# Value products with the values as weights, and group norms by transposes, in the first of two transformer blocks

## The chip, the core and the metric

The kernel runs on one core of a Trainium2 chip. The metric is the device time of one execution in microseconds (us). Engines are named as the profile names them: PE (TensorE, with PEld for its weight loads), DVE (VectorE), ACT (ScalarE), POOL (GpSimd), SP (which issues DMAs). Every engine works through its own list in order and waits at semaphores for the others.

## What is computed

Two transformer blocks over 256 tokens of width 1024, in fp32. The change lies in the first block, between its input projection and its output projection:

```python
y_sb = stick_breaking_attention(q_a, k_a, v_a)            # 4 heads of 64, causal
y_ch = chunked_relpos_attention(rms(q_b), rms(k_b), v_b)  # 8 heads of 64, softmax over earlier chunks
y_cv = short_conv_mixer(g_b, g_c, x_c)                    # 256 channels
y = group_rmsnorm(concat([y_sb, y_ch, y_cv]), w)          # groups of 64 features:
#   y * rsqrt(mean(y * y over the 64) + EPS) * w
x = x + y @ w_out
```

Both attentions end in out = A @ v for each head (A is 256 x 256 and lower triangular by blocks of 128, so the upper right block is left out). Then come a feed-forward layer and the whole second block, which the change does not touch.

## The kernel before

All weights stream from HBM in chunks of 128 x 1024 values ("slots", 8 matrix tiles each). ACT rounds each chunk to a high part (wh), DVE forms the remainder (wl), and PE multiplies three times (high by high, high by low, low by high), 24 matmuls of 256 columns a slot in most stages. A ring of 8 chunks lies between the converters and PE.

The program is written by `when(slot, prio, fn)`: for each slot the pieces of work are recorded by rising prio, and each piece appends instructions to the lists of its engines. The slot's own weight matmuls have prio 50, so what has a smaller prio stands ahead of them and what has a larger one behind. Tokens (tok) carry the semaphore counts that later pieces wait for. PSUM is eight banks of 128 x 512 fp32: M[0..2] (pm), S[0..2] (psc), T (ptr), O (po); `claim` waits for the bank's last reader.

The banded attention does one head a slot (slot SC + h and following, SC = 11): scores, row maxima on DVE, exponentials on ACT, three transposes of the probabilities into T (`ch_turn`), a copy to SBUF (`ch_keep`), and the value product (`ch_values`) into O. In it the transposed probabilities are the weights, three tiles of 128 x 128, and the values are what streams, 64 columns each time, so O holds tokens by features. Four heads fill O. `sb_values` is the same for the four causal heads, whose weights swt come from exponentials of S; before them `sb_after` multiplies softplus sums (sph, spl) with a triangle, and waits for the last of sph and spl.

The group norm of a filled O is `group_norm(part, slot, k0)`, for part 0 (heads 0 to 3), part 1 (heads 4 to 7) and part 2 (the causal heads), at slots 18, 22 and 24. `gn_take` copies O to yraw, squares it into sq, sums groups of 64 on DVE, and raises to the power -1/2 on POOL. `gn_scale` multiplies yraw by the factors on DVE. `gn_turn` transposes yraw into T (four transposes), since the output projection wants features by tokens. `gn_split` writes the high part yh (ACT, from T) and the low part yl (DVE, from T). The output projection runs in slots 24 (W1) to 31 and takes the features 2, 3, 4, 5, 0, 1 in that order, then 6 and 7 of the convolution, whose own norm (`cv_sums`, `cv_widen`, `cv_spread`, `cv_done`) already works with transposes of squares and of widened factors. Its bank S[0] is summed in slot 25, its spread in slot 27.

Of the kernel before, what the change touches and what calls it, by code (L numbers as in the profile page):

```python
# [6 lines left out]
P = 128  # L7
# [6 lines left out]
HEAD = 64  # L14
# [156 lines left out]
def build(nc, w, xt, par, cf, cb, rel, wsp, bsp, pos, fin, out):  # L171
# [3 lines left out]
    ALU = mybir.AluOpType  # L175
    ACT = mybir.ActivationFunctionType
    AX = mybir.AxisListType
# [3 lines left out]
    with ctx:  # L181
# [11 lines left out]
        def keep(name, shape, dt=fp32):  # L193
            t, top[0] = put(top[0], name, shape, dt)
            return t
# [8 lines left out]
        def sem(name):  # L204
            return ctx.enter_context(nc.semaphore(name))
# [14 lines left out]
        mhalf = keep("mhalf", [P, 16])  # L220
# [14 lines left out]
        sq = keep("sq", [P, 2, 512])  # L235
        acc = keep("acc", [P, 512])
# [3 lines left out]
        def tiny(width):  # L240
            small_n[0] += 1
            return keep(f"tiny{small_n[0]}", [P, width])
# [6 lines left out]
        gn_ss, gn_f, gn_t, gn_r = tiny(8), tiny(8), tiny(8), tiny(8)  # L249
# [49 lines left out]
        M = [Bank(pm[:, i, :]) for i in range(3)]  # L299
        S = [Bank(psc[:, i, :]) for i in range(3)]  # L300
        T, O = Bank(ptr[:, :]), Bank(po[:, :])

        pe, act, dve, pool, spq = (Lane(sem(n)) for n in ("pe", "act", "dve", "pool", "spq"))
        tok = {}

        def pairs(ap):
            return ap.rearrange("p (a n) -> p a n", a=2)
# [9 lines left out]
        def pcol(name, j):  # L317
            if name == "anw":
                return xa[:, j:j + 1]
            return parm[:, PAR[name] + j:PAR[name] + j + 1]  # L320

        def mm(dst, lhs, rhs, start, stop):
            return lambda e: e.matmul(dst, lhs, rhs, start=start, stop=stop, skip_group_check=True)  # L323

        def tr(dst, src):
            return lambda e: e.transpose(dst, src, cfs[:, CF_ID:CF_ID + P])  # L326

        def scaled(dst, src, scale):
            return lambda e: e.activation(dst, src, ACT.Copy, scale=scale)  # L329

        def func(dst, src, kind, **kw):
            return lambda e: e.activation(dst, src, kind, **kw)  # L332

        def tt(dst, a, b, op):
            return lambda e: e.tensor_tensor(dst, a, b, op)  # L335

        def stt(dst, a, s, b, op0, op1):
            return lambda e: e.scalar_tensor_tensor(dst, a, s, b, op0, op1)

        def ts(dst, a, s1, s2, op0, op1):  # L340
            return lambda e: e.tensor_scalar(dst, a, s1, s2, op0, op1)
# [4 lines left out]
        def when(slot, prio, fn):  # L346
            plan[slot].append((prio, len(plan[slot]), fn))
# [75 lines left out]
        for c in range(4):  # L423
            a = (c % 2) * 1024
            for i in range(2 if c < 2 else 1):
                b = a + (512 if c < 2 else 1024)
# [191 lines left out]
        sq_readers = {0: [], 1: []}  # L618
# [23 lines left out]
        acc_readers = []  # L642
# [215 lines left out]
        SC = VB + 3  # L858
# [47 lines left out]
        def ch_keep(h):  # L906
# [6 lines left out]
            tok["ck", h] = t  # L913
            T.release(t)

        def ch_values(h):
            after = [tok["ck", h], tok["vb", "s"]] + (O.claim() if h % 4 == 0 else [])
            c = (h % 4) * HEAD
            v = vbs[:, :, h * HEAD:h * HEAD + HEAD]
            pt = ptb[:, h % 3, :]  # L920
            pe.quiet(mm(O.ap[:, c:c + 64], pt[:, 0:P], v[:, 0, :], True, True), *after)
            pe.quiet(mm(O.ap[:, 256 + c:320 + c], pt[:, P:256], v[:, 0, :], True, False))
            tok["cp", h] = tok["pv"] = pe.do(mm(O.ap[:, 256 + c:320 + c], pt[:, 256:384], v[:, 1, :],
                                                False, True))

        for h in range(8):
            if h % 2 == 0:
# [7 lines left out]

        def gn_take(part):
            b = part % 2
            used = [tok["gt", part - 2]] if part > 1 else []
            c = act.do(func(yraw[:, b, :], O.ap, ACT.Copy), tok["pv"], *used)
            q = act.do(func(sq[:, b, :], O.ap, ACT.Square), tok["pv"], *sq_readers[b])  # L940
            O.release(q)
            tok["gy"] = c
            t = dve.do(lambda e: e.tensor_reduce(gn_ss[:, :], sq[:, b, :].rearrange(
                "p (h d) -> p h d", d=HEAD), AX.X, ALU.add), q)
            sq_readers[b] = [t]
            if part < 2:
                r = dve.do(lambda e: e.reciprocal(gn_r[:, :], den[:, 8 * part:8 * part + 8]),
                           tok["ce", 4 * part + 3])
                r2 = dve.do(tt(gn_t[:, :], gn_r[:, :], gn_r[:, :], ALU.mult), r)
                t = dve.do(tt(gn_ss[:, :], gn_ss[:, :], gn_t[:, :], ALU.mult), t, r2)  # L950
            t = dve.do(ts(gn_ss[:, :], gn_ss[:, :], 1.0 / HEAD, EPS, ALU.mult, ALU.add), t)
            tok["gf"] = pool.do(tt(gn_f[:, :], gn_ss[:, :], mhalf[:, 0:8], ALU.pow), t)

        def gn_scale(part):
            t = tok["gf"]
            if part < 2:
                t = dve.do(tt(gn_f[:, :], gn_f[:, :], gn_r[:, :], ALU.mult), t)
            v = yraw[:, part % 2, :].rearrange("p (h d) -> p h d", d=HEAD)
            tok["gn"] = dve.do(tt(v, v, gn_f[:, :].unsqueeze(2).to_broadcast([P, 8, HEAD]), ALU.mult),
                               t, tok["gy"])  # L960

        def gn_turn(part):
            after = T.claim() + [tok["gn"]]
            for pj in range(2):
                for tb in range(2):
                    f = tr(T.ap[:, pj * 256 + tb * P:pj * 256 + tb * P + P],
                           yraw[:, part % 2, tb * 256 + pj * P:tb * 256 + pj * P + P])
                    if pj and tb:
                        tok["gt", part] = pe.do(f)
                    else:  # L970
                        pe.quiet(f, *after)

        def gn_split(k0, src, ready, bank):

            for i in range(2):
                a = act.do(scaled(yh[:, k0 + i, :], src[:, i, :], pcol("onw", k0 + i)), *ready)
            for i in range(2):
                t = tok["y", k0 + i] = dve.do(stt(yl[:, k0 + i, :], src[:, i, :], pcol("onw", k0 + i),
                                                  yh[:, k0 + i, :].bitcast(fp32), ALU.mult,
                                                  ALU.subtract), a, *ready)  # L980
            if bank:
                bank.release(t)

        def group_norm(part, slot, k0, wait=0):
            when(slot, 12, lambda: gn_take(part))
            when(slot + 2, 10, lambda: gn_scale(part))
            when(slot + 2 + wait, 65, lambda: gn_turn(part))
            when(slot + 3 + wait, 11, lambda: gn_split(k0, pairs(T.ap), [tok["gt", part]], T))

        group_norm(0, SC + 7, 2, 1)  # L990
        group_norm(1, SC + 11, 4)


        def fm_out(bank, ready, dst, r, rname):
# [84 lines left out]
        def sb_values():  # L1079
            after = O.claim() + [tok["bw", 1], tok["bw", 2], tok["bw", 0], tok["va", "s"]]  # L1080
            for h in range(4):
                c, b, i = h * HEAD, h % 2, h // 2
                v = vas[:, :, c:c + HEAD]
                pe.quiet(mm(O.ap[:, c:c + 64], swt[:, b, i * 256:i * 256 + P], v[:, 0, :], True, True),
                         *after)
                pe.quiet(mm(O.ap[:, 256 + c:320 + c], swt[:, b, i * 256 + P:i * 256 + 256], v[:, 0, :],
                            True, False))
                tok["pv"] = pe.do(mm(O.ap[:, 256 + c:320 + c], swt[:, 2, h * P:h * P + P], v[:, 1, :],
                                     False, True))

        when(VA1 + 2, 62, lambda: sb_scores(0, 1))
        when(SC + 8, 62, sb_scores_last)
# [9 lines left out]
        when(SC + 10, 66, sb_after)  # L1102
        when(SC + 11, 25, sb_weights)
        when(SC + 12, 66, sb_values)
        group_norm(2, SC + 13, 0)


        def cv_x():
# [37 lines left out]
            tok["cvf"] = pool.do(tt(cv_f[:, :], cv_ss[:, :], mhalf[:, 0:8], ALU.pow), t)  # L1146

        def cv_widen():
            tok["cvw"] = act.do(func(sq[:, 0, :].rearrange("p (h d) -> p h d", d=HEAD),
                                     cv_f[:, :].unsqueeze(2).to_broadcast([P, 8, HEAD]), ACT.Copy),  # L1150
                                tok["cvf"], *sq_readers[0])

        def cv_spread():
            after = S[1].claim() + [tok["cvw"]]
            for i in range(2):
                for tb in range(2):
                    c = tb * 256 + i * P
                    f = tr(S[1].ap[:, i * 256 + tb * P:i * 256 + tb * P + P], sq[:, 0, c:c + P])
                    if i and tb:
                        tok["cvr"] = pe.do(f)  # L1160
                    else:
                        pe.quiet(f, *after)
            sq_readers[0] = [tok["cvr"]]

        def cv_done():
            t = dve.do(tt(gbs[:, :, :], gbs[:, :, :], pairs(S[1].ap), ALU.mult), tok["cvr"], tok["cvq"])
# [426 lines left out]
        for pair in range(2):  # L1593
            b = DL + 7 * pair
# [301 lines left out]
```

How the kernel before makes its waits and increments, by code:

```python
    def play(self, eng):  # L159
        passed = {}
        for fn, after, counts in self.items:
            for sem, n in after:
                if passed.get(sem.name, 0) < n:
                    eng.wait_ge(sem, n)
                    passed[sem.name] = n
            ins = fn(eng)
            if counts:
                ins.then_inc(self.sem, 1)
# [2 lines left out]
def build(nc, w, xt, par, cf, cb, rel, wsp, bsp, pos, fin, out):  # L171
# [178 lines left out]
        def load(lane, name, dst, src, *after):  # L350
            s = sem("ld_" + name)
            lane.quiet(lambda e: e.dma_start(dst, src).then_inc(s, 16), *after)
            tok[name] = (s, 16)
# [29 lines left out]
        def first_weights(lane, c, i, a, b):  # L383
            lane.quiet(lambda e: e.dma_start(raw[:, c // 2, a:b], w[c // 2, :, a:b])
                       .then_inc(s_first[c, i], 16))
# [1398 lines left out]
            for i, f in enumerate((lambda tb: out_squares(tb), lambda tb: out_gain(tb, 0), out_factor,  # L1784
                                   lambda tb: out_gain(tb, 1), out_scale)):
                when(SLOTS, 10 + 10 * tb + i, lambda f=f, tb=tb: f(tb))
        for slot, todo in enumerate(plan):
            for _, _, fn in sorted(todo, key=lambda v: v[:2]):
                fn()
        fetch(first_use, SLOTS // 2)
        for tb in range(2):
            out_store(tb)
        spq.quiet(lambda e: e.wait_ge(s_out, 64))
        block = ctx.enter_context(nc.Block())
```

## Time and profile before

| what | value |
|---|---|
| median of 3 runs | 692.37 us (692.31 to 692.38) |
| the profiled execution | 692.49 us, of it 690.7 us between its first and last instruction (the span) |
| granted clock of TensorE, mean | 0.999 of full speed |
| PE busy | 684.4 us (99%) |
| DVE, ACT, POOL busy | 463.5, 373.6, 37.4 us |
| HBM read | 122.34 MB |

A row of the chain of waits gives the start, the length and the work that the end of the kernel goes back to; since matmuls overlap, lengths there are from end to end. A row of the timeline gives one engine's instructions in a row, merged where alike; the time in a merged row is from the first start to the last end. The two numbers with a star are the part of the array that a matmul uses (rows of the array * columns).

### The profile page before, as it was taken

Reading aid. Unit: us, or ns where it says so; the run is one execution under the profiler, and the core shown is the slowest. Engines: PE = TensorE matmul, PEld = TensorE weight load, DVE = VectorE, ACT = ScalarE, POOL = GpSimd, SP = SyncE. Lnnn points to the kernel's source line nnn. Section 1 sums busy time; section 2 is a strip of 40 time slices with the busy share of each in tenths; the row PEclk is TensorE's granted clock in tenths of the full one; section 3 lists DMA queues with packets and bytes.
Section 4 is the critical chain, followed back from the end, with each engine's and each line's share of the span. In section 5 each row is a group of like instructions: output and inputs, shape, how many; then the busy total and the mean of one; then the engine's idle time right before and its main releaser. Section 6 shows DMA issues by size and latency. Waiting matters only on the chain.

```text
span 690.7 us, 12102 instructions
## 1 busy us (share of the span) xinstructions
PE 684.4 (99%) x5092; PEld 642.8 (93%) x5092; DVE 463.5 (67%) x743; ACT 373.6 (54%) x567; POOL 37.4 (5%) x33
## 2 busy tenths in 40 slices
PE   9999999999999999999999999999999999999996
PEld 7889999999999988889988898999999999998885
DVE  5975677876666654666674567558689888886422
ACT  6865765654455543556455475444467555555422
POOL 0400121300000000011000000000030000000000
PEclk9999999999999999999999999999999999999999
DMA  8953335455555565446365343434646555556501
GB/s 324 361 201 122 122 122 185 183 184 183 183 184 185 188 236 185 184 160 232 134 242 177 129 131 124 174 130 176 244 185 205 192 184 183 187 186 238 183 0 62
DMA packets 20246, 124.17 MB, mean 180 GB/s; under 512 B 2272, under 2 KB 3808, under 8 KB 5984
## 3 DMA queue, kind: packets, MB, share of 16 engines
q1 hardware_dynamic: 18000, 120.02, 48.4%
q10 hardware_dynamic: 2192, 3.38, 1.5%
q8 instruction: 40, 0.66, 0.4%
q14 instruction: 14, 0.11, 0.1%
HBM read 122.34 MB, written 1.05 MB: 179 GB/s over the span
## 4 chain that ended last, share of the span: by engine, by line
PE 98%; DMA 1%; issue 1%; ACT 0%; SPq 0%; POOLq 0%; POOL 0%; DVE 0%; ACTq 0%
PE pm L323 52%; PE psc L323 33%; PE ptr L323 8%; PE po L323 2%; PE ptr L326 1%; DMA raw<-in_w_dram 1%; PE po L326 0%; PE psc L326 0%; PE psc L1709 0%; PE pm L1709 0%; SPq L352 0%; ACT yo L329 0%; ACT sq L332 0%; ACT wh L332 0%; POOLq L181 0%
## 5 line engine op out<-in xcount | busy, mean ns | idle before, releaser
L335 DVE TENSOR_TENSOR wl<-raw,wh 128x1024 fp32r<-128x1024 f32 (+1 forms) x226 | 269.9, 1208 | 40.9 <-ACT wh L332 29.7
L332 ACT ACTIVATE wh<-raw 128x1024 fp32r<-128x1024 f32 (+1 forms) x226 | 228.4, 1036 | 54.5 <-PE psc L323 35.0
L323 PE MATMUL pm<-xh,wh 128*128 128x256 f32 x560 | 158.4, 283 | 0.0
L323 PE MATMUL pm<-xl,wh 128*128 128x256 f32 x560 | 156.3, 279 | 0.0
L323 PE MATMUL pm<-xh,wl 128*128 128x256 f32 x560 | 156.2, 279 | 0.0
L323 PEld LDWEIGHTS pm<-xh,wh 128*128 128x128 f32 x560 | 105.3, 188 | 2.8 <-issue 2.5
L323 PEld LDWEIGHTS pm<-xl,wh 128*128 128x128 f32 x560 | 105.3, 188 | 0.0
L323 PEld LDWEIGHTS pm<-xh,wl 128*128 128x128 f32 x560 | 105.3, 188 | 0.0
L323 PE MATMUL psc<-xh,wh 128*128 128x256 f32 x304 | 84.9, 279 | 0.0
L323 PE MATMUL psc<-xh,wl 128*128 128x256 f32 x304 | 84.8, 279 | 0.0
L323 PE MATMUL psc<-xl,wh 128*128 128x256 f32 x304 | 84.8, 279 | 0.0
L323 PE MATMUL pm<-wh,xh 128*128 128x512 f32 (+1 forms) x176 | 61.6, 350 | 0.0
L323 PE MATMUL pm<-wh,xl 128*128 128x512 f32 (+1 forms) x176 | 60.2, 342 | 0.0
L323 PE MATMUL pm<-wl,xh 128*128 128x512 f32 (+1 forms) x176 | 58.6, 340 | 0.0
L323 PEld LDWEIGHTS psc<-xh,wh 128*128 128x128 f32 x304 | 57.1, 188 | 0.0
L323 PEld LDWEIGHTS psc<-xl,wh 128*128 128x128 f32 x304 | 57.1, 188 | 0.0
L323 PEld LDWEIGHTS psc<-xh,wl 128*128 128x128 f32 x304 | 57.1, 188 | 0.0
L323 PE MATMUL psc<-hq,wh 128*128 128x512 f32 x132 | 46.8, 399 | 0.0
L323 PEld LDWEIGHTS pm<-wh,xh 128*128 128x128 f32 x176 | 33.3, 189 | 5.3 <-issue 1.0
L323 PE MATMUL psc<-hq,wl 128*128 128x256 f32 x132 | 37.1, 281 | 0.0
L323 PEld LDWEIGHTS pm<-wh,xl 128*128 128x128 f32 x176 | 33.4, 190 | 3.8
L323 PEld LDWEIGHTS pm<-wl,xh 128*128 128x128 f32 x176 | 33.2, 189 | 3.8
(306 smaller groups left out, 1223.7 us busy)
## 6 DMA issues: line engine op xcount, KB each, us to landing
raw<-in_w_dram SPq DMA_DIRECT2D x109, 1024.0 KB, 4.8
early<-in_w_dram SPq DMA_DIRECT2D x2, 1024.0 KB, 11.8
raw<-in_w_dram SPq DMA_DIRECT2D x2, 512.0 KB, 7.1
bias<-in_rel_dram ACTq DMA_DIRECT2D x1, 1024.0 KB, 9.1
xa<-in_xt_dram SPq DMA_DIRECT2D x3, 256.0 KB, 6.8
out_dram<-yo SPq DMA_DIRECT2D x3, 256.0 KB, 2.3
raw<-in_w_dram ACTq DMA_DIRECT2D x2, 256.0 KB, 4.2
raw<-in_w_dram SPq DMA_DIRECT2D x2, 256.0 KB, 5.5
```

The source lines that it names most:

```text
L323: return lambda e: e.matmul(dst, lhs, rhs, start=start, stop=stop, skip_group_check=True)
L326: return lambda e: e.transpose(dst, src, cfs[:, CF_ID:CF_ID + P])
L332: return lambda e: e.activation(dst, src, kind, **kw)
L335: return lambda e: e.tensor_tensor(dst, a, b, op)
```

## The change

The heads' values become the weights (64 columns of them, in the lower or the upper half of the array's columns, by `head_rows`), and the transposed probabilities stream: 256 columns for the first key block and 128 for the second. O then holds features by tokens, two heads above each other. So yraw needs no transpose, but its squares must be summed over partitions: `gn_sums` transposes the squares (four transposes, to M[2], T and S[1] for the three parts), `gn_factor` reduces them and raises to the power, `gn_widen` copies each factor over 64 columns on ACT, `gn_spread` transposes that (four transposes, to M[0], T and T), and `gn_done` multiplies yraw with it on DVE and then splits as before, now reading yraw in SBUF. The last hunk of the diff, left out here, lets the convolution's `cv_widen` and `cv_spread` use acc in place of sq for their widened factors.

```diff
@@ -913,15 +913,17 @@
             tok["ck", h] = t
             T.release(t)
 
+        def head_rows(h):
+            lo, c = 64 * (h % 2), 256 * (h // 2)
+            return O.ap[lo:lo + 64, c:c + 256]
+
         def ch_values(h):
             after = [tok["ck", h], tok["vb", "s"]] + (O.claim() if h % 4 == 0 else [])
-            c = (h % 4) * HEAD
+            dst = head_rows(h % 4)
             v = vbs[:, :, h * HEAD:h * HEAD + HEAD]
             pt = ptb[:, h % 3, :]
-            pe.quiet(mm(O.ap[:, c:c + 64], pt[:, 0:P], v[:, 0, :], True, True), *after)
-            pe.quiet(mm(O.ap[:, 256 + c:320 + c], pt[:, P:256], v[:, 0, :], True, False))
-            tok["cp", h] = tok["pv"] = pe.do(mm(O.ap[:, 256 + c:320 + c], pt[:, 256:384], v[:, 1, :],
-                                                False, True))
+            pe.quiet(mm(dst, v[:, 0, :], pt[:, 0:256], True, False), *after)
+            tok["cp", h] = tok["pv"] = pe.do(mm(dst[:, P:256], v[:, 1, :], pt[:, 256:384], False, True))
 
         for h in range(8):
             if h % 2 == 0:
@@ -935,40 +937,63 @@
 
         def gn_take(part):
             b = part % 2
-            used = [tok["gt", part - 2]] if part > 1 else []
+            used = [tok["gu", part - 2]] if part > 1 else []
             c = act.do(func(yraw[:, b, :], O.ap, ACT.Copy), tok["pv"], *used)
             q = act.do(func(sq[:, b, :], O.ap, ACT.Square), tok["pv"], *sq_readers[b])
             O.release(q)
-            tok["gy"] = c
-            t = dve.do(lambda e: e.tensor_reduce(gn_ss[:, :], sq[:, b, :].rearrange(
-                "p (h d) -> p h d", d=HEAD), AX.X, ALU.add), q)
-            sq_readers[b] = [t]
+            tok["gy", part], tok["gq", part] = c, q
+
+        def gn_sums(part, bank):
+            b, after = part % 2, bank.claim() + [tok["gq", part], tok["cf"]]
+            for i in range(2):
+                for tb in range(2):
+                    c = tb * 256 + i * P
+                    f = tr(bank.ap[:, c:c + P], sq[:, b, i * 256 + tb * P:i * 256 + tb * P + P])
+                    if i and tb:
+                        tok["gs", part] = pe.do(f)
+                    else:
+                        pe.quiet(f, *after)
+            sq_readers[b] = [tok["gs", part]]
+
+        def gn_factor(part, bank):
+            t = dve.do(lambda e: e.tensor_reduce(gn_ss[:, :], bank.ap.rearrange(
+                "p (h d) -> p h d", d=HEAD), AX.X, ALU.add), tok["gs", part])
+            bank.release(t)
             if part < 2:
                 r = dve.do(lambda e: e.reciprocal(gn_r[:, :], den[:, 8 * part:8 * part + 8]),
                            tok["ce", 4 * part + 3])
                 r2 = dve.do(tt(gn_t[:, :], gn_r[:, :], gn_r[:, :], ALU.mult), r)
                 t = dve.do(tt(gn_ss[:, :], gn_ss[:, :], gn_t[:, :], ALU.mult), t, r2)
             t = dve.do(ts(gn_ss[:, :], gn_ss[:, :], 1.0 / HEAD, EPS, ALU.mult, ALU.add), t)
-            tok["gf"] = pool.do(tt(gn_f[:, :], gn_ss[:, :], mhalf[:, 0:8], ALU.pow), t)
-
-        def gn_scale(part):
-            t = tok["gf"]
+            used = [tok["gw", part - 1]] if part else []
+            tok["gf", part] = pool.do(tt(gn_f[:, :], gn_ss[:, :], mhalf[:, 0:8], ALU.pow), t, *used)
+
+        def gn_widen(part):
+            b, t = part % 2, tok["gf", part]
             if part < 2:
                 t = dve.do(tt(gn_f[:, :], gn_f[:, :], gn_r[:, :], ALU.mult), t)
-            v = yraw[:, part % 2, :].rearrange("p (h d) -> p h d", d=HEAD)
-            tok["gn"] = dve.do(tt(v, v, gn_f[:, :].unsqueeze(2).to_broadcast([P, 8, HEAD]), ALU.mult),
-                               t, tok["gy"])
-
-        def gn_turn(part):
-            after = T.claim() + [tok["gn"]]
-            for pj in range(2):
+            tok["gw", part] = act.do(func(sq[:, b, :].rearrange("p (h d) -> p h d", d=HEAD),
+                                          gn_f[:, :].unsqueeze(2).to_broadcast([P, 8, HEAD]), ACT.Copy),
+                                     t, *sq_readers[b])
+
+        def gn_spread(part, bank):
+            b, after = part % 2, bank.claim() + [tok["gw", part]]
+            for i in range(2):
                 for tb in range(2):
-                    f = tr(T.ap[:, pj * 256 + tb * P:pj * 256 + tb * P + P],
-                           yraw[:, part % 2, tb * 256 + pj * P:tb * 256 + pj * P + P])
-                    if pj and tb:
+                    c = tb * 256 + i * P
+                    f = tr(bank.ap[:, i * 256 + tb * P:i * 256 + tb * P + P], sq[:, b, c:c + P])
+                    if i and tb:
                         tok["gt", part] = pe.do(f)
                     else:
                         pe.quiet(f, *after)
+            sq_readers[b] = [tok["gt", part]]
+
+        def gn_done(part, bank, k0):
+            y = yraw[:, part % 2, :]
+            t = dve.do(tt(y, y, bank.ap, ALU.mult), tok["gt", part], tok["gy", part])
+            bank.release(t)
+            gn_split(k0, pairs(y), [t], None)
+            tok["gu", part] = tok["y", k0 + 1]
 
         def gn_split(k0, src, ready, bank):
 
@@ -981,14 +1006,16 @@
             if bank:
                 bank.release(t)
 
-        def group_norm(part, slot, k0, wait=0):
+        def group_norm(part, slot, k0, sums, spread):
             when(slot, 12, lambda: gn_take(part))
-            when(slot + 2, 10, lambda: gn_scale(part))
-            when(slot + 2 + wait, 65, lambda: gn_turn(part))
-            when(slot + 3 + wait, 11, lambda: gn_split(k0, pairs(T.ap), [tok["gt", part]], T))
-
-        group_norm(0, SC + 7, 2, 1)
-        group_norm(1, SC + 11, 4)
+            when(slot, 64, lambda: gn_sums(part, sums))
+            when(slot + 1, 11, lambda: gn_factor(part, sums))
+            when(slot + 1, 64, lambda: gn_widen(part))
+            when(slot + 2, 64, lambda: gn_spread(part, spread))
+            when(slot + 3, 11, lambda: gn_done(part, spread, k0))
+
+        group_norm(0, SC + 7, 2, M[2], M[0])
+        group_norm(1, SC + 11, 4, T, T)
 
 
         def fm_out(bank, ready, dst, r, rname):
@@ -1080,13 +1107,9 @@
             after = O.claim() + [tok["bw", 1], tok["bw", 2], tok["bw", 0], tok["va", "s"]]
             for h in range(4):
                 c, b, i = h * HEAD, h % 2, h // 2
-                v = vas[:, :, c:c + HEAD]
-                pe.quiet(mm(O.ap[:, c:c + 64], swt[:, b, i * 256:i * 256 + P], v[:, 0, :], True, True),
-                         *after)
-                pe.quiet(mm(O.ap[:, 256 + c:320 + c], swt[:, b, i * 256 + P:i * 256 + 256], v[:, 0, :],
-                            True, False))
-                tok["pv"] = pe.do(mm(O.ap[:, 256 + c:320 + c], swt[:, 2, h * P:h * P + P], v[:, 1, :],
-                                     False, True))
+                v, dst = vas[:, :, c:c + HEAD], head_rows(h)
+                pe.quiet(mm(dst, v[:, 0, :], swt[:, b, i * 256:i * 256 + 256], True, False), *after)
+                tok["pv"] = pe.do(mm(dst[:, P:256], v[:, 1, :], swt[:, 2, h * P:h * P + P], False, True))
 
         when(VA1 + 2, 62, lambda: sb_scores(0, 1))
         when(SC + 8, 62, sb_scores_last)
@@ -1102,7 +1125,7 @@
         when(SC + 10, 66, sb_after)
         when(SC + 11, 25, sb_weights)
         when(SC + 12, 66, sb_values)
-        group_norm(2, SC + 13, 0)
+        group_norm(2, SC + 13, 0, S[1], T)
 
 
         def cv_x():
```

PE, the end of slot 21: the last banded head's value product (po), and the product with the triangle (psc<-sph,trir) that waits for spl. Before:

```order
L323 MATMUL po<-vbs,ptb 128x64 [waits act]
L323 MATMUL po<-vbs,ptb 128x64 x2
L326 MATMUL ptr<-cfs,yraw 128x128 [waits dve]
L326 MATMUL ptr<-cfs,yraw 128x128 x3
L323 MATMUL psc<-sph,trir 128x512 [waits dve]
L323 MATMUL psc<-spl,trir 128x512
L323 MATMUL psc<-sph,trir 128x512
```

Now:

```order
L323 MATMUL po<-ptb,vbs 64x256 [waits act]
L323 MATMUL po<-ptb,vbs 64x128
L323 MATMUL psc<-sph,trir 128x512 [waits dve]
L323 MATMUL psc<-spl,trir 128x512
L323 MATMUL psc<-sph,trir 128x512
L323 MATMUL psc<-spl,trir 128x512
```

The four transposes of part 0 that stood between the two have gone from here; in their place four stand at the end of slot 18 and four at the end of slot 20.

DVE, ahead of that same product with the triangle: wl is a weight conversion, sp and spl belong to the causal attention, yraw, yl are part 0 of the norm, gbs is the convolution's. Before:

```order
L335 TENSOR_TENSOR wl<-raw,wh 128x1024
L338 SCALAR_TENSOR_TENSOR sp<-psc,sp 128x512
L335 TENSOR_TENSOR spl<-sp,sph 128x512 [waits act,dve]
L338 SCALAR_TENSOR_TENSOR sp<-psc,sp 128x512
L335 TENSOR_TENSOR wl<-raw,wh 128x1024 [waits raw2]
L335 TENSOR_TENSOR spl<-sp,sph 128x512 [waits act,dve]
```

Now:

```order
L335 TENSOR_TENSOR wl<-raw,wh 128x1024
L338 SCALAR_TENSOR_TENSOR sp<-psc,sp 128x512
L335 TENSOR_TENSOR yraw<-yraw,pm 128x512 [waits pe]
L338 SCALAR_TENSOR_TENSOR yl<-yraw,parm,yh 128x256 [waits dve,act]
L338 SCALAR_TENSOR_TENSOR yl<-yraw,parm,yh 128x256
L335 TENSOR_TENSOR spl<-sp,sph 128x512
L338 SCALAR_TENSOR_TENSOR sp<-psc,sp 128x512
L335 TENSOR_TENSOR wl<-raw,wh 128x1024 [waits raw2]
L335 TENSOR_TENSOR spl<-sp,sph 128x512 [waits act,dve]
L335 TENSOR_TENSOR gbs<-pm,rbc 128x512 [waits pe]
```

The product yraw<-yraw,pm, which waits for the four transposes at the end of slot 20, and the two yl behind it, which wait for yh from ACT, now stand ahead of the last two spl; before, the yl stood behind gbs.

## Rows read from the trace of the kernel before

**Rows 1.** The page: busy time by engine; releasers of the chain that ended last.

```profile
PE 684.4 (99%) x5092; PEld 642.8 (93%) x5092; DVE 463.5 (67%) x743; ACT 373.6 (54%) x567; POOL 37.4 (5%) x33
PE 98%; DMA 1%; issue 1%; ACT 0%; SPq 0%; POOLq 0%; POOL 0%; DVE 0%; ACTq 0%
```

**Rows 2.** Waits of PE over the whole span: engine, line, releaser: total, times, longest.

```profile
PE po L323 <- POOL mhalf L361: 1.1, 1, 1.1
```

**Rows 3.** The chain, start us, length us, work: first block, 81 to 99 us.

```profile
81.74 2.80 PE pm L323 x24
84.55 0.61 PE po L323 x6
85.16 0.45 PE ptr L326 x4
85.61 2.24 PE psc L323 x14
93.49 2.62 PE po L323 x24
98.98 0.44 PE ptr L326 x4
```

**Rows 4.** Timeline of PE, second block's value products: start us, us, tile, array.

```profile
426.10 0.28 PE L323 MATMUL pm<-xh,wl 128*128 128x256 f32 x1
426.31 0.44 PE L323 MATMUL po<-pt,v2s 128*64 128x256 f32 x2
...
426.57 0.60 PE L323 MATMUL po<-pt,v2s 128*64 128x256 f32 x6
...
428.09 0.39 PE L323 MATMUL po<-pt,v2s 128*64 128x128 f32 x4
428.41 0.39 PE L323 MATMUL pm<-xh,wh 128*128 128x256 f32 x1
428.63 0.28 PE L323 MATMUL pm<-xl,wh 128*128 128x256 f32 x1
```

**Rows 5.** Timeline of PE, scores that use one array half twice running.

```profile
76.16 0.71 PE L323 MATMUL psc<-qat,kat 64*128 64x128 f32 x4
76.80 0.23 PE L323 MATMUL psc<-cbs 128*128 128x128 bf16 x1
```

**Rows 6.** Timeline of DVE around the banded attention's end.

```profile
82.18 0.69 DVE L335 TENSOR_TENSOR spl<-sp,sph 128x512 fp32r<-128x512 f32 x1 [0.92 <-ACT sph L332]
82.79 0.68 DVE L338 SCALAR_TENSOR_TENSOR sp<-psc,sp 128x512 f32<-128x512 f32 x1
83.39 1.22 DVE L335 TENSOR_TENSOR wl<-raw,wh 128x1024 fp32r<-128x1024 f32 x1
84.52 0.69 DVE L335 TENSOR_TENSOR spl<-sp,sph 128x512 fp32r<-128x512 f32 x1
86.52 0.88 DVE L338 SCALAR_TENSOR_TENSOR yl<-ptr,parm,yh 128x256 fp32r<-128x256 f32 x2
97.28 0.69 DVE L943 TENSOR_REDUCE tiny<-sq 128x8 f32<-128x512 f32 x1 [2.04 <-ACT sq L332]
98.00 0.17 DVE L341 TENSOR_SCALAR tiny<-tiny 128x8 f32<-128x8 f32 x1
110.17 0.68 DVE L335 TENSOR_TENSOR gbs<-gbs,psc 128x512 f32<-128x512 f32 x1
```

**Rows 7.** Timeline of ACT, same stretch.

```profile
83.50 0.64 ACT L332 ACTIVATE sph<-sp 128x512 fp32r<-128x512 f32 x1 [1.05 <-DVE sp L338]
85.64 0.84 ACT L329 ACTIVATE yh<-ptr,parm 128x256 fp32r<-128x256 f32 x2 [0.56 <-PE ptr L326]
105.71 0.63 ACT L332 ACTIVATE sq<-tiny 128x512 f32<-128x512 f32 x1 [3.52 <-POOL tiny L335]
```

**Rows 8.** Timeline of POOL, same stretch.

```profile
98.25 2.54 POOL L335 TENSOR_TENSOR tiny<-tiny,mhalf 128x8 f32<-128x8 f32 x1 [6.73 <-DVE tiny L341]
```

**Rows 9.** Timeline of PE at the product with the triangle.

```profile
85.36 0.48 PE L323 MATMUL psc<-sph,trir 128*128 128x512 f32 x1
```

More of the change, by code:

```diff
@@ L1148, in cv_widen @@
         def cv_widen():
-            tok["cvw"] = act.do(func(sq[:, 0, :].rearrange("p (h d) -> p h d", d=HEAD),
+            tok["cvw"] = act.do(func(acc[:, :].rearrange("p (h d) -> p h d", d=HEAD),
                                      cv_f[:, :].unsqueeze(2).to_broadcast([P, 8, HEAD]), ACT.Copy),
-                                tok["cvf"], *sq_readers[0])
+                                tok["cvf"], *acc_readers)
         def cv_spread():
@@ L1157, in cv_spread @@
                     c = tb * 256 + i * P
-                    f = tr(S[1].ap[:, i * 256 + tb * P:i * 256 + tb * P + P], sq[:, 0, c:c + P])
+                    f = tr(S[1].ap[:, i * 256 + tb * P:i * 256 + tb * P + P], acc[:, c:c + P])
                     if i and tb:
@@ L1162, in cv_spread @@
                         pe.quiet(f, *after)
-            sq_readers[0] = [tok["cvr"]]
+            acc_readers[:] = [tok["cvr"]]
         def cv_done():
```

## The prediction, as it was recorded

> **What bounds the kernel now.** I read the page first: PE is busy for 99% of the span, and the chain that ended last goes back to PE for 98% [rows 1]. Then the waits of PE: there is one of 1.1 us, at the very start [rows 2]. So from then on PE never waits for another engine, and two things alone can move the time: how long PE's own list takes, and any wait that the change brings into it. Work that is added on DVE, ACT and POOL costs nothing unless PE comes to wait for it. And whatever PE loses in the first block is not given back, as it has no idle time later to absorb it. Next I read the chain over the first block [rows 3], then single rows of PE where half of the array's columns or rows is in use [rows 4, 5], and last DVE, ACT and POOL where the norms and the causal attention meet [rows 6 to 8].
>
> **The banded value products.** Before, a head takes three fp32 matmuls of 64 columns, six records, 0.61 us of the chain [rows 3]. Now it takes two, with 256 and 128 columns and 64 columns of weights. The second block has that very form [rows 4]: twelve matmuls, six of each width, in 24 records. From the last ordinary matmul before (426.10) to the second one after (428.63) are 2.53 us; two ordinary steps of 0.117 would be 0.23, so the group costs 2.30. Its records start in pairs, one pair every 0.22 us at 256 columns and every 0.11 at 128 (six pairs of each, 1.95 together, from 426.31 to 428.41 less what the switch adds); the remaining 0.35 is the switch to half the array and back, seen as 0.21 in place of 0.117 ahead of the first record and 0.22 in place of 0.117 between the two rows behind (428.41, 428.63).
>
> The question is what a pair is. The second block's heads alternate between the lower and the upper half, so a pair may be one pass of each half, side by side. Or it is the two passes of one matmul. The scores of slot 19 use one half (there of the rows) twice running: four records of 128 columns, from 76.16 to the next at 76.80, so 0.64, of which about 0.2 is the switch: 0.11 for each record, one after the other, no pairs [rows 5]. That speaks for the first reading: a half that works alone pays each of its two passes in full. In the changed kernel a head has only one half. So a head pays 2 x 0.22 + 2 x 0.11 = 0.65, and 0.35 for the switch, which now comes with every head, as transposes or full-width products stand on both sides: 1.00 in place of 0.61. For eight heads: +3.1 us. Bounds: with the second reading 0.325 + 0.35 = 0.675 a head, +0.5; if the switch cost nothing as well, 0.325, -2.3; at the other end 0.65 + 0.45, +3.9. I take +3.1, since rows 5 are the only ones without alternation.
>
> **The causal value products.** Before: 24 records, 2.62 us [rows 3]. Now four heads in turn, lower, upper, lower, upper, each with its 256 and then its 128 columns. If the halves run side by side, the next head's wide product starts beside this head's narrow one: 4 x 0.43 + 0.22 + 0.35 = 2.3, so -0.3. Bounds: all in a row, 4 x 0.65 + 0.35 = 2.95, +0.3; second reading, 4 x 0.325 + 0.35 = 1.65, -1.0.
>
> The Trainium skill (TensorEngine Tiling, section Performance Considerations) advises just this exchange: with 64 or fewer streaming columns, swap the operands and use two column tiles, for up to twice the speed. The same page (Tiling Modes, Key Properties) says that changing the mode drains the engine, and with that the trace agrees, by the 0.35 us of rows 4. By the advice alone a head would go from 0.61 to about 0.3.
>
> **The transposes.** The norms had four each, now eight: twelve more. Four take 0.44 or 0.45 of the chain wherever they stand [rows 3], so +1.3 us. Bounds 1.2 to 1.6 (a first matmul behind them may start later).
>
> **Work off PE.** Per part, ACT gets one copy of 128x512 more (0.63, as the convolution's widening [rows 7]); DVE's scaling in SBUF becomes a product with PSUM (0.68, as the convolution's [rows 6]), and its sum reads PSUM. POOL's power stays, 2.54 us [rows 8]. No DMA moves by itself. All this costs nothing where PE is not waiting; two places are near.
>
> **The new wait at the triangle.** The product with the triangle at the end of slot 21 waits for the last spl. Before, that spl ran from 84.52 to 85.21 [rows 6] and PE started at 85.36 [rows 9]: 0.15 us to spare. Now the product yraw<-yraw,pm and two yl stand ahead of it on DVE, and they wait for the spread of part 0. Let S be the end of its four transposes, at the end of slot 20. DVE's product takes 0.03 + 0.68, ACT's two yh 0.03 + 0.84 [rows 7], DVE's two yl until the next can start 0.03 + 0.79, spl 0.61 (82.18 to 82.79), sp 0.60, the weight conversion 1.13 (83.39 to 84.52), the last spl 0.69: spl is there at S + 5.4. PE meanwhile has slot 21's matmuls, 2.80 [rows 3], and one head, 1.00, and arrives at S + 3.8. It waits 1.6 us, with the softplus and all later work behind it. The idle 0.92 that DVE had ahead of the second spl [rows 6] is the only slack there, and it goes to this. Laid out in their new order by durations like these, DVE reaches the product about 0.8 us before S and ACT reaches the yh 0.3 us before the product is done, so S does set the start; a later ACT would make the wait longer. Bounds: 0 (if S came much earlier against DVE than I think) and 2.7 (a further conversion of 1.13 in the way).
>
> **The spread of part 2.** Before, its factors were ready well ahead. Now let P be the end of the squares' transposes in slot 24. DVE must first finish part 1 (product, yl), since the four transposes of its spread end 0.44 before P: its sum for part 2 starts at P + 2.0. The power starts 0.97 later (97.28 to 98.25 [rows 6, 8]) and takes 2.54, the widening 0.63 and two steps of 0.03: P + 6.2. PE arrives after two slots of 2.80 and the convolution's transposes of 0.44, at P + 6.1. I take +0.1, with 0 and 0.8 as bounds. Part 1's yl is there 1.5 us before PE wants it.
>
> **The sum.** 3.1 - 0.3 + 1.3 + 1.6 + 0.1 = 5.8 us. On the profiled execution's own 692.49 that is 698.3; it stood 0.12 above the median of the runs, so I predict 698.2 us (+0.8%).
>
> **Rivals.** A pair is the two passes of one matmul (second reading): heads +0.5, causal -1.0, transposes +1.3, and as PE arrives 0.3 earlier at the triangle, a wait of 2.0: +2.8, 695.2. For it: the twelve matmuls of rows 4 show the same times either way. Against it: rows 5.
>
> The wait at the triangle doesn't come, because DVE has more room than I laid out, or the product isn't held by S: +4.2, 696.6. For it: it is a difference of two sums of which one has nine terms. Against it: PE had just 0.15 us to spare.
>
> More waits: a further conversion of 1.13 stands in the way at the triangle, and the spread of part 2 is late by 0.7: +7.5, 699.9. For it: both are chains over three or four engines.
>
> The other side, the change as an exchange that pays: the 64-column form costs a head its bare 0.325, because with transposes beside it the switch is hidden, and PE isn't held at the triangle. Heads -2.3, causal 1.3 - 2.62 = -1.3, transposes +1.3: -2.3, 690.1. It decides from about 0.5 us a head downwards: with the causal term in proportion, that is where heads and transposes balance. For it: there are fewer matmuls and fewer weight loads (24 in place of 36). Against it: the 0.21 and 0.22 of rows 4, and the wait. This is also what the page's advice on swapping would give, if its drain cost nothing.
>
> **How the numbers follow.** Likeliest case 0.58 (its own range 697.0 to 699.4: the switch 0.25 to 0.45, the wait 1 to 2.2), second reading 0.15, no wait 0.12, more waits 0.10, paying exchange 0.05. From 695.0 to 699.9 the range leaves out the paying exchange and the outer halves of two cases. A measurement here can tell 0.2% (1.4 us) from no change: faster by more 0.05, within it 0.02, slower 0.93.
>
> **What would show it.** In the profile after: po<-ptb,vbs at 0.9 to 1.05 us of the chain for a head, with its four records one after another and not in twos; po<-swt,vas in about 2.3 us, with pairs at the changes of head; 24 records of sq transposes; a row of waits PE psc L323 <- DVE spl of 1 to 2 us; PE busy longer by about 4 us. I am wrong if a head's records start in twos, if the chain shows heads at 0.7 or less, or if PE shows no wait near 88 us.

## The result

| | kernel before | changed kernel |
|---|---|---|
| median | 692.38 us (5 runs, 692.31 to 692.66) | 699.29 us (5 runs, 697.89 to 700.02) |
| ratio | | 1.0095, 95% interval 1.0084 to 1.0105 |
| profiled execution, span | 692.49, 690.7 | 700.02, 698.2 |
| granted clock, mean | 0.999 | 0.996 |

The change makes the kernel 6.9 us slower (+1.0%). 698.2 was predicted, with 695.0 to 699.9 as the range. The changed kernel scatters over 2.1 us: its runs at 697.89 and 698.01 have a mean clock of 0.998, the other three 0.996. The mean is a rough sign only: the traces also end at the lower clock (before, from 689.65 us of the span on), and this last stretch, 0 to 3.0 us long, moves the mean by up to 0.002.

PE's row of the page (before in [rows 1]) has 4.5 us more, busy as ever:

```profile
PE 688.9 (99%) x5080; PEld 643.0 (92%) x5080; DVE 463.0 (66%) x743; ACT 376.0 (54%) x570; POOL 36.6 (5%) x33
```

PE's waits, columns as in [rows 2], where there was one:

```profile
PE psc L323 <- DVE spl L335: 2.1, 1, 2.1
PE po L323 <- POOL mhalf L361: 1.1, 1, 1.1
PE pm L323 <- ACT wh L332: 0.6, 1, 0.6
PE ptr L326 <- ACT sq L332: 0.2, 1, 0.2
```

The first is the wait at the triangle, foreseen at 1.6 us. The second and third lie in the first 10 us, ahead of every changed instruction (the first weights landed later here, which moves the chain by 0.4 us from then on). The last is at the spread of part 2. The chain over the first block (before in [rows 3]):

```profile
66.61 0.80 PE po L323 x4
67.40 0.48 PE ptr L326 x3
...
74.39 0.45 PE pm L326 x4
...
84.75 0.45 PE pm L326 x4
...
85.23 0.70 DVE yraw L335
85.95 0.92 ACT yh L329 x2
...
86.89 0.88 DVE yl L338 x2
87.77 0.60 DVE spl L335
88.38 0.60 DVE sp L338
88.98 0.72 DVE wl L335
...
90.03 0.69 DVE spl L335
...
90.86 3.21 PE psc L323 x14
94.07 3.70 PE pm L323 x24
...
101.00 1.50 PE po L323 x16
...
105.50 0.45 PE ptr L326 x4
```

A head is 0.80, and the three transposes behind it are 0.48, where before they were 0.61 and 0.34: +0.33 a head. Four sq transposes are 0.45 each time. Then the chain leaves PE at the end of part 0's spread (85.20) and goes through the very steps of the prediction: the product yraw, two yh, two yl, spl, sp, the conversion, the last spl, 5.5 us in all (5.4 was forecast). The triangle's fourteen matmuls and the slot behind take 3.21 and 3.70 in place of 2.24 and 2.80. The causal products take 1.50 in place of 2.62.

Why the latter two stretches are so long is in the windows (stretch, its length, PE busy, granted clock, DMA share, GB/s):

```profile
88.00:90.80 2.80, 0.79 (x4) 1.00 0.07 29
92.70:96.00 3.30, 3.30 (x17) 0.54 0.51 146
96.10:98.00 1.90, 1.90 (x20) 1.00 0.66 276
```

PE is idle for 2.0 of the 2.8 us before 90.8. From 92.33 to 95.75, that is for 3.41 us, the clock is at the lower of its two levels, half of 2.4 GHz (the second window reaches 0.25 us beyond the end of it, hence 0.54 and not 0.50). At half speed 3.41 us of PE time are worth 1.7 us. The prediction had no such term.

Single records of PE, first a head, then the causal heads (in [rows 4] the second block's):

```profile
53.46 0.38 PE L323 MATMUL po<-ptb,vbs 128*64 128x256 f32 x1
```

```profile
100.93 0.88 PE L323 MATMUL po<-swt,vas 128*64 128x256 f32 x8
```

The window of the first row shows one record alone, 128x256 with 64 columns of weights: with one half in use there is nothing beside it, as [rows 5] had suggested. The head's four records start at 53.19, 53.46, 53.67 and 53.78. The causal row has 8 records in 0.88: four starts (100.93, 101.20, 101.41, 101.52), each of two records at most 0.02 us apart. The first four records have 256 columns and the next four 128. In PE's list the first head's 128-column matmul stands ahead of the second head's 256-column one, so the second head, on the other half, started before its turn in the list.

The spread of part 2 waits too:

```profile
109.42 2.55 POOL tiny L335
...
111.99 0.64 ACT sq L332
...
112.67 0.66 PE ptr L326 x4
```

POOL's power, ACT's widening, and only then the four transposes. Between the turn of part 1 before (98.98, 0.44 [rows 3]) and the spread of part 1 now (105.50) lie 6.5 us; behind the spread of part 2 they are 7.4 (before, the turn of part 2 ended at 105.90; now the spread ends at 113.33), so this stretch brought 0.9: four transposes for 0.44 and a wait of 0.5 (of which the view of waits, with its modelled ends, counts 0.2).

The sum, from these rows: 0.4 (start) + 8 x 0.33 + 1.3 (twelve transposes) - 1.0 (causal, with 0.1 of the next slot) + 2.1 + 1.7 + 0.5 = 7.6, against 7.5 in the spans. The 0.4 at the start is this execution's own.

### The profile page after: what moved, and what is told of

The parts are those of the page before. It is cut to its first block, busy times and chain, and to the rows that moved or that the text cites. A ratio compares the mean times of both kernels' runs of the same rounds, so it can differ in the third digit from the quotient of the medians.

```text
span 698.2 us, 12086 instructions
## 1 busy us (share of the span) xinstructions
PE 688.9 (99%) x5080; PEld 643.0 (92%) x5080; DVE 463.0 (66%) x743; ACT 376.0 (54%) x570; POOL 36.6 (5%) x33
## 3 DMA queue, kind: packets, MB, share of 16 engines
HBM read 122.34 MB, written 1.05 MB: 177 GB/s over the span
## 4 chain that ended last, share of the span: by engine, by line
PE 96%; DVE 1%; DMA 1%; issue 1%; ACT 1%; POOL 0%; SPq 0%; POOLq 0%; ACTq 0%
PE pm L323 51%; PE psc L323 33%; PE ptr L323 8%; PE po L323 2%; PE ptr L326 1%; DMA raw<-in_w_dram 1%; PE po L326 0%; POOL tiny L335 0%; PE psc L326 0%; DVE yl L338 0%; ACT yh L329 0%; DVE yraw L335 0%; ACT sq L332 0%; DVE spl L335 0%; PE pm L326 0%
```

## Experiments

All ratios are to the kernel before, run on the same chip in the same rounds (median 692.39 to 692.41).

**Part 0's product and split later.** One number of the order:

```diff
-            when(slot + 3, 11, lambda: gn_done(part, spread, k0))
+            when(slot + 3, 11 if part else 31, lambda: gn_done(part, spread, k0))
```

> The changed kernel with one number of the order changed: the product and split of part 0 of the norm stand behind the last spl on DVE (prio 31 in place of 11 in slot 21). Theory (the wait of 2.1 us at the triangle comes from the spread that these stand for, and the 3.4 us at half clock behind it come from the wait): both go, the last spl is there about 0.5 us before PE, time 699.3 - 2.1 - up to 1.7 = 695.5 us, granted clock 0.999. Rival 1 (the last spl is late by the softplus chain itself, pushed back by the widening on ACT): a wait of over 1 us stays, 697.5 to 699. Rival 2 (the low clock has another cause than the wait): wait gone, low clock stays, 697.2.

Measured: 695.78 us (695.64 to 696.19), ratio 1.005 (1.0037 to 1.0063), mean clock 0.998 to 0.999 in every run; the trace has no low stretch before the span's last 2 us. PE's waits, and the chain at the triangle:

```profile
PE po L323 <- POOL mhalf L361: 1.1, 1, 1.1
PE pm L323 <- ACT wh L332: 0.3, 1, 0.3
PE ptr L326 <- ACT sq L332: 0.2, 1, 0.2
```

```profile
87.45 0.80 PE po L323 x4
88.25 2.43 PE psc L323 x14
```

No wait for spl, and the triangle's matmuls follow the head at once, at 2.43. The theory holds; both rivals fall. The wait and its low clock were 3.5 us of the 6.9 (699.29 less 695.78).

**The wait filled with work that does nothing.**

```diff
         def sb_after():
+            free = T.claim()
+            for i in range(10):
+                pe.quiet(mm(T.ap[:, 0:P], ones[:, :], ones[:, :], True, True), *free)
+            T.release()
```

> The changed kernel with ten full fp32 matmuls of 128 columns on the ones, 0.22 us each, ahead of the product with the triangle; their result is not used. They fill the 2.1 us in which PE waited and save no work. Theory (the wait is what lowers the clock, and 3.4 us at half clock cost 1.7 us): granted clock 0.999 in every run, wait under 0.1 us, time 697.8 to 698.1, where the changed kernel's runs without the low clock lie (697.9, 698.0), and its scatter of 2 us gone. Rival (the low clock has another cause, as the half-array matmuls): clock 0.996 as before and time 699.3 to 699.7, or more by what the fill adds.

Measured: 698.21 us (697.94 to 698.39, 4 runs), ratio 1.0083 (1.007 to 1.0097). Its mean clock was 0.998 to 1.0, and in the trace of the profiled run, the one with 0.998, the clock is low only from 693.59 on, in the last 3 us. Chain:

```profile
87.83 0.80 PE po L323 x4
88.62 2.43 PE ptr L323 x20
91.05 2.23 PE psc L323 x14
```

The ten matmuls (twenty records) take 2.43, so the time until the triangle was wasted as before. What they give is the steady clock: the runs end within 0.5 us of where the changed kernel's two with the higher clock did, as the theory said (its 698.1 is passed by 0.1), and the scatter falls from 2.1 to 0.5 us. It is the idle PE that lowers the clock, and that is paid on top of the wait.

**The value products alone.** The kernel before with `head_rows`, the new `ch_values` and the new `sb_values`.

```diff
-            pe.quiet(mm(O.ap[:, c:c + 64], pt[:, 0:P], v[:, 0, :], True, True), *after)
-            pe.quiet(mm(O.ap[:, 256 + c:320 + c], pt[:, P:256], v[:, 0, :], True, False))
+            pe.quiet(mm(dst, v[:, 0, :], pt[:, 0:256], True, False), *after)
```

> The kernel before with the new form of both value products alone; its norms still take what they find in O as tokens by features, so the output is not the reference's. Theory (a head works on one half alone and pays each pass in full, plus 0.35 for switching; the four causal heads run side by side, two and two): banded heads +0.33 each, +2.6, causal -1.0, no new wait, so 692.4 + 1.6 = 694.0. Rival (the form itself is no slower, and what the chain of waits shows for it is a matter of how ends are modelled): 692.4 or less.

Measured: 694.0 us (693.86 to 694.38, 11 runs), ratio 1.0024 (1.0015 to 1.0033), +1.6 as expected. Chain:

```profile
66.03 0.80 PE po L323 x4
66.82 0.48 PE ptr L326 x3
...
95.92 1.50 PE po L323 x16
```

The same 0.80, 0.48 and 1.50 as in the changed kernel. The new form of the value products is by itself slower here.

**Heads in pairs.** The changed kernel, with both halves of the array in turn:

```diff
+            if h % 2 == 0:
+                return
...
+            for kb in range(2):
+                for g in (h - 1, h):
+                    v = vbs[:, kb, g * HEAD:g * HEAD + HEAD]
+                    pt = ptb[:, g % 3, 2 * kb * P:(2 + kb) * P]
+                    f = mm(head_rows(g % 4)[:, kb * P:256], v, pt, kb == 0, kb == 1)
```

> The changed kernel with the banded value products done for two heads at a time, with the lower and the upper half in turn (as the second block does it). Theory (two halves run side by side, and a group pays one switch): four groups of 0.65 + 0.35 in place of eight, so -3.8 us with the wait at the triangle and its low clock as they were: 699.3 - 3.8 = 695.5. Rival 1 (it is the switch alone that costs, halves don't overlap): four switches saved, -1.2 to -1.4: 698.0. Rival 2 (each head's own two passes could always pair, and nothing is gained): 699.3.

Measured: 696.51 us (694.74 to 697.63), ratio 1.006 (1.0047 to 1.0074): -2.8, not the full -3.8, and between the rivals' numbers, so the time alone would not have settled it. The chain does:

```profile
64.30 0.80 PE po L323 x8
65.10 0.48 PE ptr L326 x3
...
73.13 2.56 POOL tiny L335
...
75.91 0.63 ACT sq L332
76.54 0.50 ACT sp L332
...
87.33 4.50 PE psc L323 x14
```

Two heads in eight records cost 0.80, what one head cost alone: the halves do run side by side, and both rivals fall. The rest was given back at the triangle. PE came earlier, and there it found another chain: part 0's power on POOL (73.13), its widening on ACT, and only behind it the softplus of the causal attention. The wait grew from 2.1 to 2.7 us, and the half clock lasted 6.83 us in this execution (mean clock 0.994; the run at 694.74 had 0.998). It began at 86.62, while PE was still waiting (it started again at 87.33), and went on to 93.44: some 6.1 us of work at half speed, worth 3.1 us.

**A delay put into the kernel before.** The last spl is written five times over:

```diff
         def sb_low(b):
             t, a = tok["bs", b]
-            tok["bs", b] = dve.do(tt(spl[:, b, :], sp[:, b, :], sph[:, b, :].bitcast(fp32),
-                                     ALU.subtract), t, a)
+            last = []
+            for i in range(5 if b == 2 else 1):
+                tok["bs", b] = dve.do(tt(spl[:, b, :], sp[:, b, :], sph[:, b, :].bitcast(fp32),
+                                         ALU.subtract), t, a, *last)
+                last = [tok["bs", b]]
```

> The kernel before with the last spl of the causal attention written five times over on DVE, 0.61 us each, so that it comes 2.4 us later; nothing else is changed. Theory (PE had 0.15 us to spare there, and a wait of over 2 us there brings a stretch at half clock in most runs): wait of 2.3 us, runs near 694.7 where the clock holds and 696.4 or more where 3.4 us run at half clock, scatter of 1.5 us or more. Rival (the low clock belongs to the changed matmul forms): all runs within 0.5 us of 694.7.

Measured: 697.93 us (695.38 to 698.25), ratio 1.0069 (1.0056 to 1.0083). The wait is 2.6 us (the five, each waiting for the one before, cost 0.72 and not 0.61). The five runs stand in steps with their mean clock: 695.38 at 0.998, 696.67 at 0.996, 697.93, 698.17 and 698.25 at 0.994. In the profiled one the clock was low for 6.83 us, from 87.57 to 94.40; PE started again at 88.15. Windows of this run, one of the three at 0.994:

```profile
88.00:95.00 7.00, 6.85 (x28) 0.54 0.18 46
95.00:96.00 1.00, 1.00 (x11) 1.00 0.98 418
```

So with matmuls and norms in their old form a wait of 2.6 us cost between 3.0 and 5.8 us. The low clock does not belong to the changed matmuls. I had expected one step; there were two.

**The norms alone.** The changed kernel with the old `ch_values` and `sb_values`.

> The changed kernel with both value products in their old form, so that only the norms are new; they take O as features by tokens where it holds tokens by features, so the output is not the reference's. Theory (the parts add up): the changed kernel less what the value products brought (694.0 - 692.4 = 1.6), with the wait at the triangle at 2.0 to 2.4 us, as PE arrives 0.3 sooner: 697.5 to 698.3 with the low clock, 696.2 without it. Rival (value products and norms hinder each other, and the norms alone are cheap): under 694.5, that is the twelve transposes and no wait.

Measured: 698.74 us (698.56 to 699.7, 4 runs), ratio 1.0094 (1.0079 to 1.011): above the expected range by 0.4, as the wait was longer than forecast:

```profile
PE psc L323 <- DVE spl L335: 2.6, 1, 2.6
```

Norms alone +6.3, value products alone +1.6, both +6.9: 1.0 less than the sum. Half of it is the wait: the slower heads make PE late, and being late it waits 2.1 in place of 2.6 us. The clock is not shown to be the rest, as both profiled executions, the changed kernel's and this one, have one low stretch of 3.41 us (here from 89.42 to 92.83); the rest is within the scatter of the runs. Here the chain ahead of the last spl does not start at part 0's spread either: it runs through ACT's softplus (sp and sph, 79 to 83.5 us), its yh (83.87) and DVE's yl (84.70). This run also shows how little the mean clock tells: it is 0.998 in the profiled execution, with the low stretch in it, and 0.995 in the fastest run, at 698.56.

**Pairs and order.** Heads in pairs, part 0's product later, and part 2's sum ahead of part 1's product on DVE (prio 10 in place of 11).

> Heads in pairs, part 0's product and split behind the last spl, and part 2's sum ahead of part 1's product on DVE. Theory (these are the three costs, but with heads in pairs PE comes some 3 us earlier to the triangle and finds the softplus chain, which was pushed back by part 0's sum on DVE and its widening on ACT): 695.8 - 3.8 - 0.4 + a wait of about 0.6 = 692.2 us. Rival (the three simply add, no wait): 691.5. Other rival (the wait is 1.5 us or more, with low clock): 693.5 or more.

Measured: 693.06 us (692.83 to 693.43, 11 runs), ratio 1.001 (1.0001 to 1.0018). Waits:

```profile
PE pm L323 <- ACT wh L332: 1.4, 1, 1.4
PE psc L323 <- DVE spl L335: 0.8, 1, 0.8
PE pm L323 <- DVE yl L338: 0.2, 1, 0.2
```

The wait at the triangle that the theory forecast is there, with 0.8 for 0.6, and no low clock behind it. The time is 0.9 above the theory's 692.2. The 0.2 is new: part 2's low part yl is late, since on ACT its yh stands behind the convolution's widening, which waits for POOL. The 0.2 more of the wait and this new one, which the last experiments put at 0.5 us, make up most of the 0.9. The run changes three things at once and doesn't price them singly.

**Softplus first.**

```diff
-            when(slot + 1, 10 if part == 2 else 11, lambda: gn_factor(part, sums))
-            when(slot + 1, 64, lambda: gn_widen(part))
+            when(slot + 1, (31, 11, 10)[part], lambda: gn_factor(part, sums))
+            when(slot + 1, 64 if part else 67, lambda: gn_widen(part))
```

> As the one with pairs and order, and in slot 19 part 0's sum stands behind the last row maximum on DVE and its widening behind the second softplus on ACT. Theory (part 0's norm, which has time until slot 24, is what holds back the softplus chain): no wait at the triangle, 691.4 to 691.7 us, 0.8 below the kernel before: heads 4 x 1.0 in place of 8 x 0.61, causal -1.0, transposes +1.3, no waits. Rival (the sum held nothing back, the chain is bound elsewhere): as the run with pairs and order.

Measured: 692.31 us (692.11 to 692.65, 11 runs), ratio 0.9998 (0.9989 to 1.0007). Waits:

```profile
PE po L323 <- POOL mhalf L361: 1.1, 1, 1.1
PE pm L323 <- DVE yl L338: 0.2, 1, 0.2
```

The wait at the triangle is gone, so the norm of part 0 had indeed held back the softplus. The time is 0.6 above the forecast and no different from the kernel before: the last wait, counted here as 0.2, was left out of the sum, and the next run shows it to be worth 0.55.

**The convolution's widening later**, alone, and with **heads in fours**, both on top of the version before. The fours also have a fourth buffer for the transposed probabilities, left out here:

```diff
-        when(W1 + 2, 40, cv_widen)
+        when(W1 + 3, 12, cv_widen)
```

```diff
-            if h % 2 == 0:
+            if h % 4 != 3:
                 return
...
+            for i, kb in enumerate((0, 1, 0, 1)):
+                for g in (h - 3 + i // 2 * 2, h - 2 + i // 2 * 2):
```

> The version with pairs and the softplus first, with the convolution's widening on ACT behind part 2's yh alone. Theory (yh stands behind a widening that waits for POOL, and PE then waits for yl): the wait of 0.2 goes, 692.1 us. Rival (the wait only moves to the convolution's spread): 692.3.

> The version with pairs and the softplus first, further with all four heads of a bank in one group of value products (a fourth buffer for the transposed probabilities holds them until then), and with the convolution's widening on ACT behind part 2's yh. Theory (a group pays its switch once): two switches fewer, and those of the two groups left, -0.7, and the last wait of 0.2 and its tail gone: 692.3 - 0.7 - 0.2 = 691.4 us, 0.14% below the kernel before. Rival (the switch hides in what stands beside it, and only halves that run side by side matter): 692.1.

Measured, the widening alone: 691.76 us (691.54 to 691.96, 11 runs), ratio 0.9989 (0.998 to 0.9998). With fours: 691.47 us (691.12 to 692.04, 11 runs), ratio 0.9985 (0.9976 to 0.9994). Waits of the first, and the group of four heads in the chain of the second:

```profile
PE po L323 <- POOL mhalf L361: 1.1, 1, 1.1
PE pm L323 <- ACT wh L332: 0.3, 1, 0.3
```

```profile
64.01 1.45 PE po L323 x16
```

With the widening later PE waits for nothing between the first chunk and the end; it brought about 0.55 where 0.2 was expected (from 692.31 to 691.76, in different rounds whose kernel before agrees within 0.01). Four heads take 1.45 where two times two took 1.60, and the transposes behind the group that is gone take 0.33 again in place of 0.48: 0.3 for each switch saved, 0.6 for two. Half of that was given back, as PE in fours is again early at the triangle and waited 0.3 for spl. Both versions are faster than the kernel before, by 0.6 and 0.9 us (0.1%), with intervals that just leave out 1; between the two the intervals don't decide. That is the best found of this idea.

## Why the prediction came out as it did

**PE sets the time, and any wait is paid in full.** Right, and too mild: where PE waited 2.1 us or more, most runs paid again in clock.

**What it said would show.** The wait near 88 us, the four records one after another and the 4.5 us more of PE busy came as said. Two signs did not: a head is 0.80 of the chain and not 0.9 to 1.05 (with the 0.14 more of the transposes behind it, 0.94), and the causal products took 1.50 and not 2.3.

**The banded value products, +3.1.** Right in kind, 0.5 too large: +2.6. One record stands alone in its half, as read from [rows 5]. The size is off in the switch. 0.35 was taken from the second block, where ordinary full-width matmuls stand on both sides; here a head and its transposes are 1.28 of the chain, less 0.65 and 0.33 for bare work leaves 0.30.

**The causal value products, -0.3.** Mis-sized: -1.0. The prediction let the second head start beside the first one's narrow product, as if each matmul had to be taken up in turn. The 8 records in 0.88 show both heads starting together, four records of 256 columns before any of 128. [Rows 4] could not tell this, as there neighbours in the list already alternate. The lower bound of -1.0 is what came, but it was there for the second reading, whose reason was wrong: that is luck.

The Trainium skill (TensorEngine Tiling, section Tiling Modes, Key Properties) says that tiles work independently, with weight loads and matmuls in parallel; by that rule the causal heads cost 2 x 0.65 + 0.35 = 1.65 against 1.50 on the chain, and the trace agrees. The same page of the Trainium skill (section Performance Considerations) advises to swap the operands and tile the columns where 64 or fewer columns stream. In this case that came true only for the causal heads (1.50 for 2.62) and for the pairs and fours (0.80 for two heads, where they were 0.61 each), where both tiles have work. For a head alone the runs speak against it (0.80 for 0.61).

**The transposes, +1.3.** Right: 0.44 to 0.45 for four.

**The wait at the triangle, +1.6.** The mechanism was right step by step. Measured 2.1: PE came 3.6 behind the spread in place of 3.8 (this head is 0.80, with no transposes behind it), the last spl 5.5 behind it in place of 5.4, and PE took 0.14 to start.

**What failed by omission: the clock.** "Bounds: 0 ... and 2.7" for this wait leaves out what an idle PE does to the speed behind it. It was worth 1.7 us in the profiled execution, the third largest term after the heads (2.6) and the wait itself (2.1). The filled wait (clock steady, 698.21) and the delay in the kernel before (steps with the clock) show it from both sides. That the forecast of 698.2 still came within 1.1 us is in part luck: it was 1.2 too high on the causal and the banded products together, and 2.6 too low on the clock (1.7), the wait (0.5) and the spread (0.4), all read from the profiled execution, which is 0.7 above the median.

**The spread of part 2, +0.1.** A wait, as worked out, of 0.5 and not 0.1. It lay within its bounds (0 to 0.8). The prediction's own terms give PE's arrival as P + 6.0 (two times 2.80 and 0.44), not 6.1, so 0.2 would have been its sum.

**The rivals.** The second reading is refuted (single records), "no wait" too. "More waits", at 699.9, named the right places but not the clock. The paying exchange did not come with this change. It exists, but only with both halves in use and an order that lets the softplus pass, and then it pays 0.9 us.

## What to carry to other kernels

In this case half an array's columns gained nothing unless the other half had a matmul to run beside it: look for single records or twos in the trace, and group heads so that halves alternate. When an addition puts a new chain on DVE or ACT, write out what stands between it and the next wait of the engine that bounds; with 0.15 us to spare, one norm's product and two yl put ahead of it cost 3.5 us. And where PE bounds, don't price a wait of over 2 us at its bare length: here the waits of 2.1 and 2.6 us cost from 1.0 to 2.2 times theirs (the changed kernel's runs less 695.78, the delay's less 692.41), in seven runs of ten over 1.5 times. Avoid such a wait; filling it saved at most what the clock would have cost.

## What the runs showed of the hardware that was not expected

- Around a wait of PE of 2.1 to 2.7 us the granted clock went to the lower level for 3.41 us (changed kernel, norms alone) or 6.83 us (heads in pairs, delay in the kernel before) in the profiled executions. The 3.41 began after PE had gone back to work, by 1.5 us in the changed kernel (90.86 to 92.33) and 0.8 us with the norms alone; the 6.83 began while PE still waited, 0.7 and 0.6 us before its end. What decides between the two is not shown. Not every run seems to have a low stretch, by the times: the runs of the changed kernel, of the pairs and of the delay differ by 2.1 to 2.9 us. With waits of 0.8 us or less at the triangle, no profile had such a stretch, nor did one follow the waits of up to 1.4 us in the first 10 us.
- Two heads whose matmuls follow each other in the list, each two matmuls long and each on its own half, start together (100.93 and 100.94 in the changed kernel, where the matmul that stands between them in the list starts at 101.41): a half does not wait for the other's turn.
- DVE operations of 128x512 that each wait for the one before came every 0.72 us (five in 3.59 us), in place of 0.61.
